# A two-block network: the wait for mixed rows taken block by block, and a next part's first row worked on at another point

## Chip, cores and metric

The kernel runs on one core of one Trainium2 chip. The metric is the device time in microseconds of one execution. Several engines work side by side on the core: TensorE (PE in the profile; its weight loads are PEld) multiplies, VectorE (DVE), ScalarE (ACT) and GpSimd (POOL) do elementwise work, SyncE (SP) issues most transfers. Each runs its own list of instructions in order, and they wait for one another through semaphores.

## What is computed

The program is two blocks one behind the other over 512 tokens of width 1024: a gated linear-attention and retention block, then a two-layer block (convolution, windowed attention). Each of those two layers ends in the part that the change touches, a gated feed-forward with 2816 hidden channels:

```python
def swiglu_ffn(x, w_up, w_down):
    gate, up = jnp.split(x @ w_up, 2, axis=-1)
    return (jax.nn.silu(gate) * up) @ w_down
...
        h = h + swiglu_ffn(rmsnorm(h, norm_ffn[l]), ffn_w_up[l], ffn_w_down[l])
    return rmsnorm(h, norm_final)
```

## The kernel before

**Products by seven instead of eight.** A float32 product is made of three passes: each operand is split into a high part (a cast) and a low part (the value less its high part), and high by high, high by low and low by high are added up. In the feed-forward the work is further cut by a Strassen-like scheme. A *pair* is a 2 by 2 block of output (two output chunks of 128 channels, two token halves of 256). `seven_products` (L2568) computes it with seven products, named `w11`, `diff`, `sum2`, `w12`, `sum1`, `w22` and `sum4`, instead of eight. Each product is 4 blocks (`HALF`) of 3 matmuls of 128x256, so 12 matmuls, and a pair is 84. Some products need sums or differences of weight blocks (made by VectorE and GpSimd), and sums or differences of input blocks, which are called *mixes*.

**Order of the pairs.** `ff_order` (L48) gives 30 pairs per layer. The 22 hidden chunks come in three parts of 8, 8 and 6. For part 0: up pairs for its chunks 0 to 7 (pairs 0 to 7), then the first up pair of the next part (pair 8), then four down pairs (9 to 12), which multiply the part's eight finished hidden chunks by the down weights. Then up pairs 13 to 19, first up pair of part 2 (pair 20), down pairs 21 to 24, up pairs 25 to 29. Part 2 goes through ordinary dense products at the end. Pairs of even number use the PSUM tensor `aps`, those of odd number `gps`.

**What a pair needs from the other engines.** ScalarE walks the same pairs (L1252 on). For pair n it casts the weights of pair n+1 (L1094, L1106, L1100, L1117, L1111), and copies four partial results of pair n out of PSUM (`copied`, L1121, steps 1 to 4). TensorE signals `product_done` for each step and waits for the copies through `partial_copied`: step 1 before `sum2`, step 3 before `sum1`, step 4 before `sum4`. Between the copies ScalarE does the silu of pair n-1 (L1214) and the high part of its hidden row (L1221, L1231 or L1235). VectorE's turn for pair n-1 is `gate_and_up` (L1975 to L1980) or `down_added` (L1986 to L1993); then it makes the low weight sums (L1845, L1850, L1855) and the next weight sums (L1838, L1840). GpSimd makes the low weights (L740, L743, L744, L746, L748).

**Hidden mixes.** After an odd hidden chunk, ScalarE casts the mixes of the two chunks (`hidden_mix_high`, L1246) and GpSimd subtracts for the low part (`hidden_mix_low`, L761, semaphore `hid_mix_low`). A part has four such mix blocks, m = 0 to 3; block 3 comes from chunks 6 and 7, that is behind pair 7. GpSimd does it behind its weights for pair 9. The products `diff` and `sum2`, `sum1` and `w22` of a down pair read them. Before pair 9 (and 21) TensorE waits for all four:

```python
if n == lead_down:
    pe.wait_ge(hid_low, mixed_at(layer_n, part + 1, 0))
    pe.wait_ge(hid_mix_low, mixes_before(layer_n, part + 1))
```

**The next part's first row.** The hidden row of pair 8 (or 20) belongs to the next part, whose first place in memory is still read by the down pairs. So it is only copied aside (`row_copy`, L1221), and worked on once the four down pairs are through: `early_high` (L1237; L1239 128x256 at the end of part 0, L1241 128x512 at the end of part 1) on ScalarE, `early_low` (L2030; L2037 and L2039, or L2034) on VectorE. Both stand at the end of the turn of pair 13 (or 25).

With two layers of two such changes of part there are four places of the first kind (pairs 9 and 21) and four of the second (pairs 13 and 25), each twice.

## Time and profile before

| | us |
|---|---|
| median of 3 runs | 1593.33 |
| lowest and highest | 1592.66, 1594.79 |
| the profiled execution, as timed | 1594.84 |
| its span in the trace | 1593.1 |
| TensorE busy | 1548.4 (97%) |
| VectorE busy | 1138.3 (71%) |
| GpSimd busy | 883.4 (55%) |
| ScalarE busy | 881.9 (55%) |

The span is 1.74 us shorter than the profiled execution's own time. The feed-forward stages lie at about 730 to 1045 us and 1235 to 1555 us of the trace. A matmul's shown length (0.28 us) is a modelled end of a pipelined instruction; the pace is read from the distance of the starts. The idle time in brackets runs from the modelled end of the matmul before. The granted clock is given as a share of 2.4 GHz.

### The profile page before, as it was taken

The page shows a single profiled execution, that of the slowest core. Times are in us where ns is not written, and L with a number is a line of the kernel's source. Part 1 is how long each engine was busy: PE and PEld are TensorE (multiplying, and loading weights), DVE is VectorE, ACT ScalarE, POOL GpSimd, SP SyncE. Part 2 cuts the span into 40 slices and gives each one's busy share as a digit, 9 for nine tenths or more (in the row PEclk, how much of TensorE's full clock was granted, in tenths as well). Part 3 has the DMA queues.
Part 4 walks back from the last instruction along what each step waited for, and adds up shares of the span by engine and source line. Part 5 has one row for each costly group of instructions (what it writes and reads, how often), then busy time and mean ns, then how long its engine had stood idle before and what let it go on. Part 6 is the DMA issues. An engine that isn't in the chain of part 4 may idle for free.

```text
span 1593.1 us, 28481 instructions
## 1 busy us (share of the span) xinstructions
PE 1548.4 (97%) x10803; PEld 1376.7 (86%) x10803; DVE 1138.3 (71%) x1782; ACT 881.9 (55%) x1480; POOL 883.4 (55%) x523
## 2 busy tenths in 40 slices
PE   6999999999999999999999999999999999999997
PEld 4888888888887878478999999988788899999996
DVE  7887687697697869877666766664666766766655
ACT  4555445455456544476664664554776665565553
POOL 1444444444445439736766776654116677677653
PEclk9999999999999999999999999999999999999999
DMA  9423322322323365612333333353112233332332
GB/s 375 139 93 88 111 93 79 118 92 81 117 92 114 114 129 148 180 53 81 106 93 106 93 106 107 105 173 103 44 41 82 92 106 107 94 105 93 106 118 69
DMA packets 53659, 173.12 MB, mean 109 GB/s; under 512 B 5403, under 2 KB 11580, under 8 KB 53052
## 3 DMA queue, kind: packets, MB, share of 16 engines
q1 hardware_dynamic: 47296, 159.90, 31.6%
q10 hardware_dynamic: 6268, 11.95, 3.3%
q8 instruction: 59, 0.97, 0.3%
q14 instruction: 36, 0.29, 0.1%
HBM read 165.48 MB, written 6.36 MB: 108 GB/s over the span
## 4 chain that ended last, share of the span: by engine, by line
PE 74%; DVE 6%; issue 4%; ACT 2%; POOL 2%; DVEq 0%; ACTq 0%; POOLq 0%
PE gps L2151 8%; PE gps L2153 8%; PE gps L2152 8%; PE gps L2586 8%; PE gps L2588 8%; PE gps L2587 8%; PE aps L2586 4%; PE aps L2587 4%; PE aps L2588 4%; PE gps L2511 2%; PE gps L2209 1%; PE gps L2210 1%; PE gps L2211 1%; POOL w_lo L665 1%; PE aps L2675 1%
## 5 line engine op out<-in xcount | busy, mean ns | idle before, releaser
L665 POOL TENSOR_TENSOR w_lo<-w_raw,w_hi 128x1024 fp32r<-128x1024 f32 x140 | 360.7, 2580 | 472.5 <-ACT w_hi L791 472.4
L2151 PE MATMUL gps<-xa_hi,w_hi 128*128 128x512 f32 x639 | 256.5, 401 | 3.9 <-DVE xa_lo L1453 3.9
L2153 PE MATMUL gps<-xa_hi,w_lo 128*128 128x512 f32 x639 | 249.8, 391 | 0.0
L2152 PE MATMUL gps<-xa_lo,w_hi 128*128 128x512 f32 x639 | 249.8, 391 | 0.0
L791 ACT CAST w_hi<-w_raw 128x1024 fp32r<-128x1024 f32 x140 | 146.3, 1045 | 98.5 <-DMA w_raw<-weights_dram 41.8
L2151 PEld LDWEIGHTS gps<-xa_hi,w_hi 128*128 128x128 f32 x639 | 120.4, 188 | 31.4 <-DVE xa_lo L1453 5.2
L746 POOL TENSOR_TENSOR w_lo<-diff,w_hi 128x512 fp32r<-128x512 f32 x60 | 77.7, 1295 | 124.0 <-ACT w_hi L1117 124.0
L2153 PEld LDWEIGHTS gps<-xa_hi,w_lo 128*128 128x128 f32 x639 | 120.3, 188 | 26.2
L1855 DVE TENSOR_TENSOR sums<-aps,sums 128x512 fp32r<-128x512 f32 x58 | 40.1, 692 | 142.1 <-ACT sums L1111 142.1
L2152 PEld LDWEIGHTS gps<-xa_lo,w_hi 128*128 128x128 f32 x639 | 120.6, 189 | 22.8
L740 POOL TENSOR_TENSOR w_lo<-w_raw,w_hi 128x512 fp32r<-128x512 f32 x60 | 91.0, 1517 | 44.8 <-ACT w_hi L1094 44.8
L2151 PE MATMUL gps<-xb_hi,w_hi 128*128 128x512 f32 x250 | 98.4, 394 | 0.0
L2153 PE MATMUL gps<-xb_hi,w_lo 128*128 128x512 f32 x250 | 97.4, 389 | 0.0
L2152 PE MATMUL gps<-xb_lo,w_hi 128*128 128x512 f32 x250 | 97.3, 389 | 0.0
L1845 DVE TENSOR_TENSOR sums<-aps,sums 128x1024 fp32r<-128x1024 f32 x58 | 70.7, 1219 | 26.5 <-ACT sums L1106 26.2
L743 POOL TENSOR_TENSOR diff<-w_raw 128x512 f32<-128x512 f32 x60 | 79.6, 1327 | 0.0
L744 POOL TENSOR_TENSOR w_lo<-w_raw,w_hi 128x512 fp32r<-128x512 f32 x60 | 78.7, 1311 | 0.0
L748 POOL TENSOR_TENSOR w_lo<-w_raw,w_hi 128x512 fp32r<-128x512 f32 x60 | 78.0, 1300 | 0.0
L2586 PE MATMUL gps<-x_blocks,w_hi 128*128 128x256 f32 x264 | 75.5, 286 | 0.0
L2588 PE MATMUL gps<-x_blocks,w_lo 128*128 128x256 f32 x264 | 74.7, 283 | 0.0
L2587 PE MATMUL gps<-x_blocks,w_hi 128*128 128x256 f32 x264 | 74.7, 283 | 0.0
L2209 PE MATMUL gps<-w_hi,xa_hi 128*128 128x256 f32 x256 | 72.8, 284 | 1.8 <-POOL w_lo L665 1.7
(495 smaller groups left out, 5135.4 us busy)
## 6 DMA issues: line engine op xcount, KB each, us to landing
w_raw<-weights_dram SPq DMA_DIRECT2D x268, 512.0 KB, 3.6
ada_w<-ada_in_dram SPq DMA_DIRECT2D x8, 1024.0 KB, 18.5
gates<-ret_tab_dram ACTq DMA_DIRECT2D x4, 1024.0 KB, 6.8
spread<-glu_scratch_dram SPq DMA_DIRECT2D x12, 270.0 KB, 5.1
rel_scratch_dram<-rel_rows ACTq DMA_DIRECT2D x1, 3072.0 KB, 34.6
x<-x_turned_dram SPq DMA_DIRECT2D x2, 1024.0 KB, 7.4
res<-xT_dram ACTq DMA_DIRECT2D x1, 2048.0 KB, 10.6
bias<-rel_scratch_dram ACTq DMA_DIRECT2D x1, 2048.0 KB, 9.5
```

The lines of the kernel that those rows point to most:

```text
L665: TT(w_lo[:, j, :], w_raw[:, j, :], w_hi[:, j, :].bitcast(F32), ALU.subtract).then_inc(lo_ready[j], 1)
L740: TT(lo["w11"], raw["w11"], hi["w11"].bitcast(F32), ALU.subtract).then_inc(first_low, 1)
L743: TT(diff[:], raw["w11"], raw["diff"], ALU.subtract).then_inc(diff_made, 1)
L744: TT(lo["w12"], raw["w12"], hi["w12"].bitcast(F32), ALU.subtract).then_inc(lo_ready[2 * s], 1)
L791: nc.scalar.copy(w_hi[:, j, :], w_raw[:, j, :]).then_inc(hi_ready[j], 1)
L2151: mm(gps[:, j, :], w_hi[:, j, w], x[0][:, k, :], start=k == 0, stop=False)
L2152: mm(gps[:, j, :], w_hi[:, j, w], x[1][:, k, :], start=False, stop=False)
L2153: last = mm(gps[:, j, :], w_lo[:, j, w], x[0][:, k, :], start=False, stop=k == blocks - 1)
L2209: mm(out, x[0][:, k, tok], wh, start=k == 0, stop=False)
L2586: mm(out, highs[s][name][:, w], x[name](k, 0), start=start and k == 0, stop=not start, **more)
L2587: mm(out, highs[s][name][:, w], x[name](k, 1), start=False, stop=not start, **more)
L2588: last = mm(out, lows[s][name][:, w], x[name](k, 0), start=False, stop=not start or k == HALF - 1, **more)
```

## The change

It has two parts.

First, `seven_products` gets an argument `mixes`. For the first down pair of a part (9 and 21) it holds how many mixes were there before the part, and each block k of `diff` waits for mix k alone. The wait for all mixes ahead of the pair goes. And, as was so already for the very first pair of a layer (`lead`), `diff` and `sum2` are cut behind their third block: three blocks of `diff`, three of `sum2`, then the last of `diff`, then the last of `sum2`. `product_done` for step 2 is now signalled behind the last block of `diff`, so 33 matmuls into the pair instead of 24; that for step 3 stays at 36.

Second, `early_high` moves from the end of ScalarE's turn for pair 13 (25) to between its copies 2 and 3, and `early_low` from the end of VectorE's turn, behind the weight sums for the pair after next, to ahead of `last_sum_low`.

```diff
--- before.py
+++ after.py
@@ -1267,6 +1267,9 @@
                     copied(f, 2, hbuf[:, 2 * s + 1, TH:], UP_SUM[s])
                     if kind == "up":
                         hidden_high(1 - s, part, k)
+                    if kind == "down" and k == KC // 2 - 1:
+                        act.wait_ge(tile_done[2 * (1 - s) + 1], up + (n - 1) // 2 + 2)
+                        early_high(part + 1)
                     copied(f, 3, hbuf[:, 2 * s + 1, 0:TH], UP_ROW[s])
                     if n == 0:
                         act.wait_ge(sq_used, USED[norm] + 4)
@@ -1282,9 +1285,6 @@
                     if n == 0:
                         rms_finish(norm, bank=NORM_BANK)
                         first_copy(f + 1, I1, s1)
-                    if kind == "down" and k == KC // 2 - 1:
-                        act.wait_ge(tile_done[2 * (1 - s) + 1], up + (n - 1) // 2 + 2)
-                        early_high(part + 1)
                     if kind == "up" and part < MIXED_PARTS and k % 2 == 1:
                         hidden_mix_high(f - 1, part, k // 2)
                 kind, part, k = FF_ORDER[-1]
@@ -2052,12 +2052,12 @@
                         last_sum(f + 1, 1 - s)
                     if kind == "up":
                         hidden_low(1 - s, part, k)
+                    if kind == "down" and k == KC // 2 - 1:
+                        early_low(part + 1)
                     if n + 1 < FF_PAIRS:
                         last_sum_low(f + 1, 1 - s)
                     if n + 2 < FF_PAIRS:
                         two_sums(up + (n + 2) // 2, f + 2, s)
-                    if kind == "down" and k == KC // 2 - 1:
-                        early_low(part + 1)
                 kind, part, k = FF_ORDER[-1]
                 gate_and_up(FF_PAIRS - 1, part, k)
                 hidden_low((FF_PAIRS - 1) % 2, part, k)
@@ -2565,7 +2565,7 @@
                         "diff": lambda k, h: mix[:, 1, k, h, :], "w22": lambda k, h: mix[:, 2, k, h, :],
                         "sum2": lambda k, h: mix[:, 3, k, h, :]}
 
-            def seven_products(f, I, s, x, lead=None):
+            def seven_products(f, I, s, x, lead=None, mixes=None):
 
                 def input_made(name, k):
 
@@ -2582,6 +2582,8 @@
                     for k in range(k0, k1):
                         if lead is not None:
                             input_made(name, k)
+                        if mixes is not None and name == "diff":
+                            pe.wait_ge(hid_mix_low, mixes + k + 1)
                         w = slice(k * P, (k + 1) * P)
                         mm(out, highs[s][name][:, w], x[name](k, 0), start=start and k == 0, stop=not start, **more)
                         mm(out, highs[s][name][:, w], x[name](k, 1), start=False, stop=not start, **more)
@@ -2597,14 +2599,15 @@
                     pe.wait_ge(block_ready, KC * lead + KC - 2)
                 product("w11", UP_ROW[s], start=True).then_inc(product_done, 1)
                 pe.wait_ge(diff_low, f + 2)
-                split = HALF - 1 if lead is not None else HALF
+                in_turn = lead is not None or mixes is not None
+                split = HALF - 1 if in_turn else HALF
                 last = product("diff", UP_SUM[s], start=True, k1=split)
-                if lead is None:
+                if not in_turn:
                     last.then_inc(product_done, 1)
                 pe.wait_ge(partial_copied, 4 * f + 1)
                 pe.wait_ge(sum_low, 2 * f + 1)
                 last = product("sum2", UP_ROW[s], k1=split)
-                if lead is not None:
+                if in_turn:
                     product("diff", UP_SUM[s], start=True, k0=split).then_inc(product_done, 1)
                     last = product("sum2", UP_ROW[s], k0=split)
                 last.then_inc(product_done, 1)
@@ -2639,9 +2642,9 @@
                     for n in range(lead_down // 2 * 2, last_down // 2 * 2 + 2):
                         if n == lead_down:
                             pe.wait_ge(hid_low, mixed_at(layer_n, part + 1, 0))
-                            pe.wait_ge(hid_mix_low, mixes_before(layer_n, part + 1))
                         kind, _, _ = FF_ORDER[n]
-                        seven_products(f0 + n, up + n // 2, n % 2, own_x if kind == "down" else x)
+                        seven_products(f0 + n, up + n // 2, n % 2, own_x if kind == "down" else x,
+                                       mixes=mixes_before(layer_n, part) if n == lead_down else None)
                     at = last_down // 2 + 1
                 quads(at, FF_PAIRS // 2)
                 n = FF_PARTS[-1]
```

No instruction is added or removed but waits. Line numbers behind L1269 shift by 3 at most (L2586 to L2588 become L2588 to L2590). These are rows of the order in which the instructions stand on an engine.

TensorE at the start of pair 9 of the first layer, before (two rows of pair 8 first, `hid_bottom` and `hid_top` are the hidden rows, `xa_mix` the mixes):

```order
L2587 MATMUL gps<-x_blocks,sums 128x256
L2588 MATMUL gps<-x_blocks,sums 128x256
L2586 MATMUL gps<-hid_bottom,w_hi 128x256 [waits evicted2,evicted3,rows_free,first_low,hid_mix_low,hid_low]
L2587 MATMUL gps<-hid_bottom,w_hi 128x256
L2588 MATMUL gps<-hid_bottom,w_lo 128x256
L2586 MATMUL gps<-hid_top,w_hi 128x256
```

After, from the end of `w11` into `diff`:

```order
L2589 MATMUL gps<-hid_top,w_hi 128x256
L2590 MATMUL gps<-hid_top,w_lo 128x256
L2588 MATMUL gps<-xa_mix,w_hi 128x256 [waits hid_mix_low,diff_low]
L2589 MATMUL gps<-xa_mix,w_hi 128x256
L2590 MATMUL gps<-xa_mix,w_lo 128x256
L2588 MATMUL gps<-xa_mix,w_hi 128x256 [waits hid_mix_low]
L2589 MATMUL gps<-xa_mix,w_hi 128x256
```

The wait `hid_mix_low` stands no longer at the first matmul of `w11` but at each block of `diff`.

TensorE in the same pair, where `diff` (`w_hi`, `w_lo`) ends and `sum2` (`sums`) begins, before:

```order
L2588 MATMUL gps<-xa_mix,w_lo 128x256
L2586 MATMUL gps<-xa_mix,w_hi 128x256
L2587 MATMUL gps<-xa_mix,w_hi 128x256
L2588 MATMUL gps<-xa_mix,w_lo 128x256
L2586 MATMUL gps<-xa_mix,sums 128x256 [waits sum_low,partial_copied]
L2587 MATMUL gps<-xa_mix,sums 128x256
```

After, from the end of `sum2`'s third block through the two last blocks to `w12`:

```order
L2589 MATMUL gps<-xa_mix,sums 128x256
L2590 MATMUL gps<-xa_mix,sums 128x256
L2588 MATMUL gps<-xa_mix,w_hi 128x256 [waits hid_mix_low]
L2589 MATMUL gps<-xa_mix,w_hi 128x256
L2590 MATMUL gps<-xa_mix,w_lo 128x256
L2588 MATMUL gps<-xa_mix,sums 128x256
L2589 MATMUL gps<-xa_mix,sums 128x256
L2590 MATMUL gps<-xa_mix,sums 128x256
L2588 MATMUL gps<-hid_bottom,w_hi 128x256 [waits lo_ready2]
```

The fourth block of `diff`, with its wait, stands behind three blocks of `sum2`.

ScalarE in the turn of pair 13 (first layer), from its first copy to the weights for pair 15, before:

```order
L1121 COPY gps<-gps 128x256 [waits product_done,evicted1]
L1106 CAST sums<-aps 128x1024 [waits sum_made,tile_done1]
L1121 COPY hbuf<-gps 128x256 [waits product_done] x2
L1100 CAST w_hi<-w_raw 128x512 [waits tile_done1,raw_in1]
L1117 CAST w_hi<-diff 128x512 [waits tile_done1,diff_made]
L1121 COPY gps<-gps 128x256 [waits product_done]
L1111 CAST sums<-aps 128x512 [waits sum_made]
L1239 CAST hid_bottom<-hbuf 128x256 [waits tile_done1]
L1094 CAST w_hi<-w_raw 128x1024 [waits tile_done2,raw_in2]
```

After:

```order
L1121 COPY gps<-gps 128x256 [waits product_done,evicted1]
L1106 CAST sums<-aps 128x1024 [waits sum_made,tile_done1]
L1121 COPY hbuf<-gps 128x256 [waits product_done]
L1239 CAST hid_bottom<-hbuf 128x256 [waits tile_done1]
L1121 COPY hbuf<-gps 128x256 [waits product_done]
L1100 CAST w_hi<-w_raw 128x512 [waits tile_done1,raw_in1]
L1117 CAST w_hi<-diff 128x512 [waits tile_done1,diff_made]
L1121 COPY gps<-gps 128x256 [waits product_done]
L1111 CAST sums<-aps 128x512 [waits sum_made]
```

The cast L1239 moved ahead of the third copy (the second `hbuf<-gps` copy).

VectorE in the same turn, with the rows taken away and put in:

```order
 L1845 TENSOR_TENSOR sums<-aps,sums 128x1024 [waits sum_high]
 L1850 TENSOR_TENSOR aps<-w_raw,aps 128x512 [waits sum_low]
-L1855 TENSOR_TENSOR sums<-aps,sums 128x512 [waits sum_high]
-L1838 TENSOR_TENSOR aps<-w_raw 128x512 [waits sum_low,raw_in2,raw_in3]
-L1840 TENSOR_TENSOR aps<-aps,w_raw 128x512 [waits sum_made]
 L2037 TENSOR_TENSOR hid_bottom<-hbuf,hid_bottom 128x256 [waits hid_high]
 L2039 TENSOR_TENSOR hbuf<-hbuf 128x256 [waits hid_low]
+L1855 TENSOR_TENSOR sums<-aps,sums 128x512 [waits sum_high]
+L1838 TENSOR_TENSOR aps<-w_raw 128x512 [waits sum_low,raw_in2,raw_in3]
+L1840 TENSOR_TENSOR aps<-aps,w_raw 128x512 [waits sum_made]
 L1975 TENSOR_TENSOR sq<-gps,rstd 128x512 [waits tile_done3]
```

The two instructions of `early_low` stand now ahead of the low part of the last weight sum (L1855) and of the sums for pair 15 (L1838, L1840), and `gate_and_up` of pair 13 (L1975) follows these sums directly.

## Rows read from the trace of the kernel before

**Rows 1.** page, section 1: busy us, share of the span, instructions

```profile
PE 1548.4 (97%) x10803; PEld 1376.7 (86%) x10803; DVE 1138.3 (71%) x1782; ACT 881.9 (55%) x1480; POOL 883.4 (55%) x523
```

**Rows 2.** waits of TensorE: total us, times, longest us

```profile
PE gps L2586 <- issue: 7.6, 4, 1.9
...
PE aps L2586 <- ACT gps L1121: 3.8, 5, 1.2
```

**Rows 3.** TensorE's timeline, first place: start, length, instruction, [idle before, its releaser]

```profile
823.63 0.28 PE L2588 MATMUL gps<-x_blocks,sums 128*128 128x256 f32 x1
825.81 0.36 PE L2586 MATMUL gps<-hid_bottom,w_hi 128*128 128x256 f32 x1 [1.90 <-issue]
...
826.60 0.38 PE L2586 MATMUL gps<-hid_top,w_hi 128*128 128x256 f32 x1
...
830.14 0.28 PE L2588 MATMUL gps<-xa_mix,w_lo 128*128 128x256 f32 x1
...
837.45 0.28 PE L2586 MATMUL aps<-hid_bottom,w_hi 128*128 128x256 f32 x1
```

**Rows 4.** timeline of GpSimd and ScalarE at the first place

```profile
822.96 2.75 POOL L761 TENSOR_TENSOR xa_mix<-hbuf,xa_mix 128x1024 fp32r<-128x1024 f32 x1 [0.73 <-ACT xa_mix L1246]
...
824.86 0.63 ACT L1214 ACTIVATE sq<-sq 128x512 f32<-128x512 f32 x1 [1.03 <-DVE sq L1975]
```

**Rows 5.** stretches of 15 us: length, TensorE busy (matmuls), clock, DMA share, GB/s

```profile
900.00:915.00 15.00, 15.00 (x127) 1.00 0.28 89
823.00:838.00 15.00, 13.10 (x97) 0.89 0.30 85
949.00:964.00 15.00, 13.10 (x98) 0.89 0.31 87
1329.00:1344.00 15.00, 13.10 (x109) 1.00 0.35 107
...
880.00:895.00 15.00, 13.77 (x115) 1.00 0.24 71
```

**Rows 6.** timeline of ScalarE in the pair before the first place

```profile
815.37 0.36 ACT L1121 COPY gps<-aps 128x256 f32<-128x256 f32 x1
...
818.20 0.37 ACT L1121 COPY hbuf<-aps 128x256 f32<-128x256 f32 x1 [0.58 <-PE aps L2588]
```

**Rows 7.** timeline of VectorE at the second place

```profile
872.32 0.69 DVE L1850 TENSOR_TENSOR aps<-w_raw,aps 128x512 f32<-128x512 f32 x1
875.99 0.69 DVE L1855 TENSOR_TENSOR sums<-aps,sums 128x512 fp32r<-128x512 f32 x1 [2.98 <-ACT sums L1111]
...
877.55 0.70 DVE L1840 TENSOR_TENSOR aps<-aps,w_raw 128x512 f32<-128x512 f32 x1
878.16 0.78 DVE L2037 TENSOR_TENSOR hid_bottom<-hbuf,hid_bottom 128x256 fp32r<-128x256 f32 x1
878.97 1.40 DVE L2039 TENSOR_TENSOR hbuf<-hbuf 128x256 f32<-128x256 f32 x1
880.30 0.68 DVE L1975 TENSOR_TENSOR sq<-gps,rstd 128x512 f32<-128x512 f32 x1
```

**Rows 8.** timeline of ScalarE at the second place

```profile
870.77 0.37 ACT L1121 COPY hbuf<-gps 128x256 f32<-128x256 f32 x1
872.22 0.37 ACT L1121 COPY hbuf<-gps 128x256 f32<-128x256 f32 x1 [1.07 <-PE gps L2588]
...
881.54 0.36 ACT L1121 COPY gps<-aps 128x256 f32<-128x256 f32 x1
```

**Rows 9.** timeline of GpSimd at the second place

```profile
873.70 1.29 POOL L746 TENSOR_TENSOR w_lo<-diff,w_hi 128x512 fp32r<-128x512 f32 x1 [2.60 <-ACT w_hi L1117]
```

**Rows 10.** instructions of one line: min/median/max ns; and one undisturbed subtraction

```profile
L1239 ACT CAST hid_bottom<-hbuf x2: 418/418/418, 875.8 to 1380.8; 128x256 fp32r<-128x256 f32 x2
...
L1241 ACT CAST xa_hi<-hbuf x1: 634/634/634, 1001.9 to 1001.9; 128x512 fp32r<-128x512 f32 x1
...
808.81 0.41 DVE L2025 TENSOR_TENSOR hbuf<-aps,hbuf 128x256 f32<-128x256 f32 x1
```

## The prediction

> **What bounds the kernel now.** I read the busy shares first. TensorE is busy 97% of the span, VectorE 71%, the others 55% [rows 1]. So in the feed-forward nothing is gained but where TensorE stands still or runs slow. Next I read TensorE's waits. Two groups in the feed-forward's line stand out: four waits of 1.9 us each, 7.6 us, put down to "issue", and five for ScalarE's copy L1121, 3.8 us, the longest 1.2 us [rows 2].
>
> The timeline shows what the first group is. Pair 8 ends with a matmul that starts at 823.63; the first of pair 9 starts at 825.81 [rows 3]. GpSimd's last mix (L761) runs from 822.96 to 825.71 [rows 4], so the wait ends 0.10 us behind it. It is the wait for the mixes, whatever the profile calls it. The undisturbed pace is 127 matmuls in 15 us, 0.12 us from start to start [rows 5], so the next matmul was due at 823.75 and came 2.06 us late.
>
> The stall is not the whole loss. From 826.60 to 830.14 there are 17 matmuls, 0.21 us apart [rows 3], and the granted clock of that stretch of 15 us is 0.89 on the mean [rows 5]: for some 3.5 us TensorE ran at the lower of its two levels, 1.2 GHz in place of 2.4. It had stood idle 1.9 us just before. A pair of 84 matmuls should take 84 x 0.12 = 10.08 us; pair 9 took from 823.75 to 837.45, 13.70 us [rows 3], so 3.6 us too long.
>
> The same in counts: the stretch at the first place holds 97 matmuls where 127 fit, 30 x 0.12 = 3.60 us lost. The second place lost 29 x 0.12 = 3.48 us. The third, whose clock stayed at 1.00, lost 18 x 0.12 = 2.16 us [rows 5]. The fourth (1454 to 1469 us) has the count and the clock of the second, 3.48 us. Together **12.7 us**, of which about 4.2 us is the slow clock.
>
> **First part: the wait by blocks.** Removed: the wait ahead of `w11`. With it gone pair 9 can start at 823.75. The rows of `w11`, 12 matmuls, last until 825.19, and three blocks of `diff` until 823.75 + 21 x 0.12 = 826.27. Mixes 0 to 2 were made two or more pairs ago. Three blocks of `sum2` last until 827.35, and only there is mix 3 needed. It is ready at 825.71 [rows 4]: GpSimd's L761 hangs on ScalarE's cast of the mixes and on pair 9's weights, neither of which waits for this stall. 1.6 us to spare, so the price of the new waits is nothing. Were the cover gone, each microsecond of a later mix beyond these 1.6 would come back.
>
> What is late next? Three things, in the order in which TensorE meets them.
> - The first copy, due at 826.27 instead of 826.63, because `sum2` now comes three matmuls earlier. ScalarE's silu of pair 8 starts at 824.86 and takes 0.63 [rows 4]. In pair 8, which started 10.08 us before, at 813.67, the copy started at 815.37, 1.70 us in, and took 0.36 [rows 6]. The same in pair 9 gives 825.45 to 825.81. Spare: 0.46 us.
> - The third copy. Step 2 is signalled 33 matmuls into the pair, at 827.71, instead of 24; step 3 at 36 as before. In pair 8 the third copy started 0.21 us behind its signal (813.67 + 4.32 = 817.99; 818.20 [rows 6]). With the same lag copy 2 starts at 827.92, takes 0.37, then comes the row copy of 128x512, for which I take the cast of that size, 0.63 [rows 10], then copy 3, 0.37: ready at 829.29. `sum1` is due at 823.75 + 48 x 0.12 = 829.51. Spare: 0.22 us, the tightest. I take 0 and keep 0 to 0.3 us a place, 1.2 us in all, as the upper end.
> - The weights of pair 10, due at 833.83 and behind. GpSimd starts them at 825.7 as it does now, since it did not wait for TensorE there. The low part of `diff` needs ScalarE's casts behind copy 3, so 829.3 + 1.25 (two casts of 0.63), then 1.3 on GpSimd [rows 9]: 831.9, needed at 835.27. No price.
>
> No DMA is issued at another point; the queue's share is 0.30 in these stretches against 0.28 in an undisturbed one [rows 5], so a pair that comes 3.6 us sooner is no load.
>
> With the idle time gone the slow clock should go: in these rows it follows the 1.9 us of idling at three of four places. So I take the whole 12.7 us. The bounds: 12.7 - 4.2 = 8.5 if the low clock stayed, and 13.2 above, since a count is good to one matmul, 0.12 us at each of four places.
>
> **Second part: the first row moved.** In pair 14 (start 837.45 + 4 x 10.08 = 877.77) `sum2` is due at 880.65. The first copy ran from 881.54 to 881.90 [rows 8]. ScalarE did it behind the silu, and that hangs on VectorE's L1975, which started only at 880.30, behind L2037 and L2039 [rows 7]. These took 0.78 and 1.40 us beside busy GpSimd, where a subtraction of the same size takes 0.41 [rows 10]. Cost: the stretch from 880 holds 115 matmuls of 127, 12 x 0.12 = 1.44 us [rows 5], and the second layer has the same count (1385 to 1400 us): 2.88 us.
>
> Moved ahead, the two instructions fall into VectorE's hole from 873.01 (end of L1850) to 875.99, 2.98 us [rows 7]. Their input is ready: ScalarE's cast, 0.42 (0.63 in the larger form) [rows 10], comes behind copy 2, whose end is 871.14, and copy 3 did not start before 872.22 [rows 8], so it fits in ScalarE's own hole of 1.07 and is done by 871.8 at the latest. The two instructions last between 2 x 0.41 = 0.82 and 2.14 (878.16 to 880.30, the old place). GpSimd starts L746 at 873.70 [rows 9], after the first of them; I take about 1.2, and both ends fit. Then L1855, L1838 and L1840 keep their times, L1975 starts at 878.16 in place of 880.30, and the copy ends at 881.90 - 2.14 = 879.76, 0.89 us before it is due. The wait goes whole.
>
> A page says more on that neighbourhood. The Trainium skill, SBUF — State Buffer, Who interferes with whom, has a VectorE instruction with two SBUF inputs and a GpSimd instruction that reads SBUF exclude each other for a whole instruction. The trace agrees in kind (0.78 and 1.40 against 0.41). By the rule both could wait for a GpSimd instruction of 1.3 us each, 3.4 us in all, 0.4 beyond the hole; that is inside the 0.89 us to spare, so the sum stays, and only the margin shrinks.
>
> The two places at the end of part 1 lose little: 3.8 us less 2 x 1.2 leaves 1.4 us for three waits [rows 2], not all of them there. I take 0.1 each, 0.2; the bounds are 0 and 1.4.
>
> **Sum.** 12.7 + 2.9 + 0.2 = 15.8 us. The profiled execution took 1594.84 us, so 1579.0. It is 1.5 us above the median of the runs shown (1593.33), and I give the forecast against the median: **1577.5 us**, 0.990 of before. As 0.2% (3.2 us) is about what a measurement can tell, this is well outside.
>
> **The rivals.**
> 1. *The low clock stays.* The drop is not tied to this idle time but comes again within the stage, near each change of part. For: it came at only three of four equal stalls, so something beside the stall decides. Against: outside these stalls the stretches show 1.00, also where TensorE waited 1.2 us (880 to 895) [rows 5]. Price: the first place lost 12 matmuls' time more than the third, 1.44 us; three of them 4.3 us: 1581.8 us.
> 2. *ScalarE's chain in pair 9 is late.* 0.22 us to spare before `sum1`, 0.46 before `sum2`. If a signal or a copy takes 0.5 us more than I think, TensorE stops 0.3 us at each place; and if the row copy waits for VectorE, more. Price 1 to 3 us: 1579.5 us.
> 3. *The change does not do what it says.* The 1.9 us end with something else that comes at the same time as mix 3, so pair 9 still stands. Against: the end 0.10 us behind L761. The second part alone leaves 1593.3 - 3.1 = 1590.2 us.
> 4. *Slower.* The pauses are what lets the clock stay high: a TensorE that works without a pause gets the lower level from time to time in the 60 pairs. Each such episode costs 1.44 us, so it decides from 11 more than now (15.8 / 1.44). One in every third pair is 20 x 1.44 = 28.8 us: 1606.3 us. Against: 15 us with all 127 matmuls at 1.00 [rows 5], and the drops stand behind idling, not behind work. The Trainium skill, TensorE: Matmul & The Clock Gate, Part 1, says that activity releases the throttle and that its peak-current limit does not trip with one or two busy cores; here one core is busy and the rows agree, which is why I give this little.
>
> **How the numbers follow.** The forecast, all stalls and drops gone: 0.76. Rival 1: 0.09. Rival 2: 0.08. Rival 3: 0.03. Rival 4: 0.04. The forecast's own spread is the runs' (the three shown span 2.1 us) and the ends of the terms (upper end 1.2 us for the chain, 1.2 us of gain for the later second places). The range reaches from 1575.0 over rivals 1 and 2 to 1583.0 us and leaves out rivals 3 and 4 and a little of the rest. Faster by over 0.2%: 0.76 + 0.09 + 0.08 = 0.93. Within 0.2%: rival 3, 0.03. Slower: rival 4, 0.04.
>
> **What would show it right or wrong.** In the trace of the changed kernel the four waits of 1.9 us before a down pair are gone, and any matmul of pair 9 that waits names a block of `diff` or the copies. Stretches around these places hold about 127 matmuls in 15 us at a clock of 1.00. VectorE's L2037 and L2039 stand in front of L1855, last 0.8 to 2.1 us, and L1855 has less idle time in front; L1975 follows L1840 with no gap, and pair 14 has no wait before `sum2`. TensorE's busy time falls by about the slow clock's 4 us, and the rest of the gain is idle time. The prediction is wrong if the fourth block of `diff` waits for L761, if copy 3 of pair 9 starts later than about 5.3 us into the pair, or if low-clock stretches show up between pairs with no stall before them.

## The result

| | median us | lowest to highest | runs |
|---|---|---|---|
| before | 1592.99 | 1592.02 to 1594.79 | 4 |
| changed | 1578.05 | 1576.66 to 1578.58 | 4 |

The ratio is 0.9904, with a 95% interval from 0.9886 to 0.9921: faster by 14.9 us. A second comparison gave 0.991 [0.9893, 0.9926]. The forecast was 1577.5 us, in a range from 1575.0 to 1583.0.

The profiled execution of the changed kernel took 1578.51 us, its span is 1576.7 us, 16.4 us shorter than before. The page's first section (busy us, share, instructions) answers [rows 1]:

```profile
PE 1544.0 (98%) x10803; PEld 1372.8 (87%) x10803; DVE 1134.5 (72%) x1782; ACT 881.7 (56%) x1480; POOL 884.3 (56%) x523
```

TensorE is busy for 4.4 us less, for the same number of instructions. That this equals what the slow clock cost is chance. Within the two feed-forward stages the busy time fell by 6.4 us, from 616.1 to 609.7. Of that 4.4 us are the slow clock, and 2.0 us are modelled ends of matmuls and slow first steps at the waits that went. The stages ahead of the first feed-forward were 1.9 us busier. The idle time within the two stages fell by 10.4 us, from 14.9 to 4.5. So the two stages are 16.8 us shorter, and the others 0.4 us longer. TensorE's waits (total, times, longest), beside [rows 2]:

```profile
PE gps L2588 <- ACT hbuf L1121: 2.9, 2, 1.5
...
PE aps L2588 <- ACT gps L1121: 1.0, 1, 1.0
```

The four waits of 7.6 us put down to "issue" are gone from the list, and of the five for the copy into `gps` one is left, at the start of a layer, with which the change has nothing to do. The first row, a wait of 1.46 us in pair 1 of each layer, was there before too.

The stretches of 15 us around the four places of the first kind and, last, one of the second kind (length, TensorE busy, matmuls, granted clock, DMA share, GB/s), beside [rows 5]:

```profile
820.00:835.00 15.00, 15.00 (x127) 1.00 0.39 117
945.00:960.00 15.00, 15.00 (x128) 1.00 0.28 100
1325.00:1340.00 15.00, 15.00 (x128) 1.00 0.34 105
1450.00:1465.00 15.00, 15.00 (x127) 1.00 0.42 132
874.00:889.00 15.00, 15.00 (x127) 1.00 0.33 106
```

Each holds the 127 or 128 matmuls that an undisturbed stretch held, where before there were 97, 98, 109 and 98, and 115 in the stretches that the prediction counted. The clock is 1.00.

**Inside pair 9.** GpSimd's last mix and TensorE's starts of `w11`, `diff` and the fourth block of `diff`:

```profile
823.35 2.82 POOL L761 TENSOR_TENSOR xa_mix<-hbuf,xa_mix 128x1024 fp32r<-128x1024 f32 x1 [0.72 <-ACT xa_mix L1246]
```

```profile
824.14 0.28 PE L2588 MATMUL gps<-hid_bottom,w_hi 128*128 128x256 f32 x1
...
825.58 0.28 PE L2588 MATMUL gps<-xa_mix,w_hi 128*128 128x256 f32 x1
...
827.74 0.28 PE L2588 MATMUL gps<-xa_mix,w_hi 128*128 128x256 f32 x1
```

The pair begins 0.12 us behind pair 8's last start, the mix is ready at 826.17 and first needed at 827.74: 1.57 us to spare, the prediction had 1.64. ScalarE's copies 1, 2, the row copy and copy 3 of that pair:

```profile
825.84 0.36 ACT L1121 COPY gps<-gps 128x256 f32<-128x256 f32 x1
...
828.30 0.37 ACT L1121 COPY hbuf<-gps 128x256 f32<-128x256 f32 x1 [1.18 <-PE gps L2590]
828.57 0.59 ACT L1221 COPY hbuf<-aps 128x512 f32<-128x512 f32 x1
829.05 0.39 ACT L1121 COPY hbuf<-gps 128x256 f32<-128x256 f32 x1
```

Copy 3 is through at 829.44. `sum1` was due 48 matmuls in, at 824.14 + 5.76 = 829.90. So 0.46 us were to spare, where the prediction had 0.22 (copy 1, through at 826.20 and needed at 826.66, had the 0.46 foretold): the row copy takes 0.59 instead of 0.63, and the next copy starts before the one in front is through.

**Inside pairs 13 and 14.** VectorE, beside [rows 7], ScalarE, beside [rows 8], and GpSimd, beside [rows 9]:

```profile
869.69 0.42 DVE L2037 TENSOR_TENSOR hid_bottom<-hbuf,hid_bottom 128x256 fp32r<-128x256 f32 x1
870.14 0.42 DVE L2039 TENSOR_TENSOR hbuf<-hbuf 128x256 f32<-128x256 f32 x1
872.76 0.69 DVE L1855 TENSOR_TENSOR sums<-aps,sums 128x512 fp32r<-128x512 f32 x1 [2.19 <-ACT sums L1111]
873.59 0.70 DVE L1838 TENSOR_TENSOR aps<-w_raw 128x512 f32<-128x512 f32 x1
874.32 0.70 DVE L1840 TENSOR_TENSOR aps<-aps,w_raw 128x512 f32<-128x512 f32 x1
874.93 0.68 DVE L1975 TENSOR_TENSOR sq<-gps,rstd 128x512 f32<-128x512 f32 x1
```

```profile
867.81 0.41 ACT L1239 CAST hid_bottom<-hbuf 128x256 fp32r<-128x256 f32 x1
...
876.24 0.36 ACT L1121 COPY gps<-aps 128x256 f32<-128x256 f32 x1
```

```profile
870.47 1.29 POOL L746 TENSOR_TENSOR w_lo<-diff,w_hi 128x512 fp32r<-128x512 f32 x1 [2.60 <-ACT w_hi L1117]
```

L2037 and L2039 take 0.42 each instead of 0.78 and 1.40, in a hole in which GpSimd is idle but for the last 0.1 us. L1855 has 2.19 us of idling left in front. L1975 stands right behind L1840. The first copy of pair 14 ends at 876.60, 0.82 us before `sum2` is due (pair 14 starts at 824.14 + 5 x 10.08 = 874.54; + 2.88 = 877.42).

### The profile page after: what moved, and what is told of

Read it like the earlier page. It is cut to its first block, busy times and chain, and to the rows that moved or that the text cites. A ratio compares the mean times of both kernels' runs of the same rounds, so it can differ in the third digit from the quotient of the medians.

```text
span 1576.7 us, 28481 instructions
## 1 busy us (share of the span) xinstructions
PE 1544.0 (98%) x10803; PEld 1372.8 (87%) x10803; DVE 1134.5 (72%) x1782; ACT 881.7 (56%) x1480; POOL 884.3 (56%) x523
## 4 chain that ended last, share of the span: by engine, by line
PE 79%; DVE 3%; issue 2%; ACT 2%; POOL 2%; DVEq 0%; ACTq 0%; POOLq 0%
PE gps L2151 9%; PE gps L2153 9%; PE gps L2152 9%; PE gps L2588 8%; PE gps L2590 8%; PE gps L2589 8%; PE aps L2588 4%; PE aps L2589 4%; PE aps L2590 4%; PE gps L2511 2%; PE gps L2209 2%; PE gps L2210 1%; PE gps L2211 1%; POOL w_lo L665 1%; PE aps L2678 1%
## 5 line engine op out<-in xcount | busy, mean ns | idle before, releaser
L665 POOL TENSOR_TENSOR w_lo<-w_raw,w_hi 128x1024 fp32r<-128x1024 f32 x140 | 361.1, 2584 | 472.5 <-ACT w_hi L791 472.4
L1855 DVE TENSOR_TENSOR sums<-aps,sums 128x512 fp32r<-128x512 f32 x58 | 40.1, 692 | 138.4 <-ACT sums L1111 138.4
L740 POOL TENSOR_TENSOR w_lo<-w_raw,w_hi 128x512 fp32r<-128x512 f32 x60 | 92.7, 1545 | 41.6 <-ACT w_hi L1094 41.5
L1845 DVE TENSOR_TENSOR sums<-aps,sums 128x1024 fp32r<-128x1024 f32 x58 | 70.8, 1221 | 17.1 <-ACT sums L1106 16.8
L743 POOL TENSOR_TENSOR diff<-w_raw 128x512 f32<-128x512 f32 x60 | 78.5, 1308 | 0.0
L748 POOL TENSOR_TENSOR w_lo<-w_raw,w_hi 128x512 fp32r<-128x512 f32 x60 | 78.1, 1301 | 0.0
L2588 PE MATMUL gps<-x_blocks,w_hi 128*128 128x256 f32 x264 | 75.5, 286 | 0.0
L2590 PE MATMUL gps<-x_blocks,w_lo 128*128 128x256 f32 x264 | 74.7, 283 | 0.0
```

Of the source, the lines that this page charges most:

```text
L665: TT(w_lo[:, j, :], w_raw[:, j, :], w_hi[:, j, :].bitcast(F32), ALU.subtract).then_inc(lo_ready[j], 1)
L740: TT(lo["w11"], raw["w11"], hi["w11"].bitcast(F32), ALU.subtract).then_inc(first_low, 1)
L743: TT(diff[:], raw["w11"], raw["diff"], ALU.subtract).then_inc(diff_made, 1)
L2588: mm(out, highs[s][name][:, w], x[name](k, 0), start=start and k == 0, stop=not start, **more)
L2590: last = mm(out, lows[s][name][:, w], x[name](k, 0), start=False, stop=not start or k == HALF - 1, **more)
```

## Experiments

Every kernel was timed beside the kernel before on the same chip, and ratios are to that. Times of different calls differ by a microsecond or two beyond the medians, since the stages ahead of the feed-forward vary: the first matmul of the first feed-forward's pair 0 starts between 727.3 and 733.0 us in the traces. So what the traces show between two matmuls is the finer measure. "Lost" below is the time that a pair took, from the last start of the pair ahead to its own last start, over 84 x 0.12 us. It holds the wait and the slower first steps behind it: a wait that the prediction counts as 2.06 us between two starts is 2.13 us lost.

### The two parts by themselves

The first kernel has the first part alone: `early_high` and `early_low` stand where they were before.

```diff
@@ ScalarE's and VectorE's turns, against the changed kernel
-if kind == "down" and k == KC // 2 - 1:
-    act.wait_ge(tile_done[2 * (1 - s) + 1], up + (n - 1) // 2 + 2)
-    early_high(part + 1)
 copied(f, 3, hbuf[:, 2 * s + 1, 0:TH], UP_ROW[s])
...
+if kind == "down" and k == KC // 2 - 1:
+    act.wait_ge(tile_done[2 * (1 - s) + 1], up + (n - 1) // 2 + 2)
+    early_high(part + 1)
...
-if kind == "down" and k == KC // 2 - 1:
-    early_low(part + 1)
 if n + 1 < FF_PAIRS:
     last_sum_low(f + 1, 1 - s)
 if n + 2 < FF_PAIRS:
     two_sums(up + (n + 2) // 2, f + 2, s)
+if kind == "down" and k == KC // 2 - 1:
+    early_low(part + 1)
```

> The first part of the change alone: the mixes waited for block by block with the two last blocks at the end; the next part's first row is worked on in its old place. Theory (the two parts remove different waits and their gains add): the wait before the down pair and its slow clock are gone, 12.9 us, and pair 14's wait of 1.2 us stays in each layer, 3.0 us with its pace. Time 1578.05 + 3.1 = 1581.1 us, two waits of about 1.2 us for ScalarE's copy before sum2 in pair 14, none before pair 9, granted clock 1.00 around pair 9. Rival (a pair that starts 3.6 us sooner runs into the same late row, so the parts don't add and the old wait grows): over 1583 us, the waits before sum2 longer than 1.5 us.

Measured: 1583.86 us (1582.16 to 1584.61), ratio 0.9928 [0.9909, 0.9947]. TensorE's waits for the copy:

```profile
PE aps L2588 <- ACT gps L1121: 3.8, 5, 1.2
```

The same as [rows 2] to the digit: five, the longest 1.2 us. Lost in pair 14: 1.48 us in each layer, as before; in pair 26: 0.44 us, as before; none ahead of pairs 9 and 21. The wait did not grow, and the trace bears out the theory of two independent waits. The median by itself lies in the rival's range, but the kernel before took 1595.29 us beside it, and 0.9928 of 1592.99 is 1581.5 us, the theory's figure.

The second kernel has the second part alone: the wait for all four mixes stands ahead of `w11` again.

```diff
 pe.wait_ge(hid_low, mixed_at(layer_n, part + 1, 0))
+pe.wait_ge(hid_mix_low, mixes_before(layer_n, part + 1))
...
-               mixes=mixes_before(layer_n, part) if n == lead_down else None)
+               mixes=None)
```

> The second part of the change alone: the next part's first row is worked on in the new place, all four mixes are waited for before the down pair as before. Theory: 1592.99 - 3.1 = 1589.9 us; four waits of 1.9 us stay, the waits of 1.2 us in pair 14 are gone, the slow clock still comes behind most of the four waits. Rival (the gain of this part is taken back since the long wait before had given the other engines time): no difference from before, 1592 to 1593.5 us.

Measured: 1589.97 us (1586.67 to 1593.55), ratio 0.9964 [0.9948, 0.998]. The ratio makes this 5.7 us, and the theory's 3.1 us (0.998) lies at the edge of the interval. Its stretches around the four places of the first kind and one of the second:

```profile
820.00:835.00 15.00, 13.10 (x110) 1.00 0.30 92
945.00:960.00 15.00, 13.11 (x110) 1.00 0.31 102
1325.00:1340.00 15.00, 13.10 (x110) 1.00 0.29 90
1450.00:1465.00 15.00, 13.11 (x110) 1.00 0.29 105
874.00:889.00 15.00, 15.00 (x128) 1.00 0.44 129
```

The waits in pair 14 are gone (128 matmuls from 874). The four waits of 1.9 us are there, 2.1 us lost at each. But 110 matmuls, not 97, and the clock is 1.00 at all four: in this execution it did not fall at any of them. So the stall does not bring the low clock each time, and the question was open how much of the 12.7 us of the first part is the chip's chance. Its span, 1586.6 us, is 6.5 us under that of before: 3.9 us for the second part's places and 4.4 us of low clock, less 1.9 us by which its first feed-forward began later.

### Is the cut of diff needed?

```diff
@@
-    in_turn = lead is not None or mixes is not None
+    in_turn = lead is not None
```

> The changed kernel without the cut: each block of diff waits for its own mix, but diff is done whole, four blocks, and then sum2, as in every other down pair. Theory (the wait ahead of w11 was the whole matter, and w11 with three blocks of diff is cover enough): mix 3 is ready at 826.17 in the trace after, the fourth block of diff would be due at 824.14 + 21 x 0.12 = 826.66, so nothing waits: 1578 us, within 0.2% of the changed kernel, no wait in pair 9. Rival (the cut is needed): a wait for GpSimd's mix of up to 0.5 us in each of four pairs, 1580 us, and more where the clock falls behind it.

Measured: 1578.56 us (1576.87 to 1579.3), ratio 0.989 [0.987, 0.9909], the same as the change. GpSimd's last mix, and TensorE at the start of `diff`'s fourth block:

```profile
824.19 2.80 POOL L761 TENSOR_TENSOR xa_mix<-hbuf,xa_mix 128x1024 fp32r<-128x1024 f32 x1 [0.72 <-ACT xa_mix L1246]
```

```profile
827.50 0.28 PE L2588 MATMUL gps<-xa_mix,w_hi 128*128 128x256 f32 x1
```

Ready at 826.99, needed at 827.50: 0.51 us to spare, and nothing waits. The two last blocks at the end add cover that the wait by blocks does not need. The cut's gain is nothing, and it costs nothing either. The two places where the prediction saw little to spare, the first and the third copy, are places that the cut itself moves closer: in this trace they end 0.82 and 0.87 us before they are needed, with the cut 0.46 and 0.46.

### How late must the wait stand?

```diff
@@
-                pe.wait_ge(hid_mix_low, mixes + k + 1)
+                pe.wait_ge(hid_mix_low, mixes + HALF)
@@
-    in_turn = lead is not None or mixes is not None
+    in_turn = lead is not None
```

> As the one without the cut, but the first block of diff waits for all four mixes. So TensorE waits 12 matmuls later than in the kernel before. Theory: diff is due at 824.14 + 1.44 = 825.58, mix 3 is there at 826.17 + 0.10: a wait of 0.7 us at each of four places, 2.8 us, 1580.9 us, and if the low clock follows only idling as long as 1.9 us, the clock stays at 1.00. Rival (any idling at this place brings the low clock, as at three of four places before): 1.4 us more at three or four places, 1585 to 1586.5 us.

Measured: 1585.25 us (1581.33 to 1586.38), ratio 0.9929 [0.9908, 0.9951]. The median lies at the rival's figure, the ratio (0.9929 of 1592.99 is 1581.7 us) and the trace at the theory's. The last matmul of `w11` and the first of `diff`:

```profile
829.19 0.28 PE L2590 MATMUL gps<-hid_top,w_lo 128*128 128x256 f32 x1
830.02 0.36 PE L2588 MATMUL gps<-xa_mix,w_hi 128*128 128x256 f32 x1 [0.54 <-POOL xa_mix L761]
```

0.76 to 0.78 us lost at each of the four places, 3.1 us, no low clock in any. In this trace the first feed-forward began 3.7 us later than in the changed kernel's, and that and the 3.1 us make up the whole difference of the two spans, 6.8 us. Most of the 3.7 us is one wait ahead of the feed-forward, for GpSimd's `w_lo` (L665): 5.0 us in all in this trace, 1.7 in the changed kernel's. The edit does not touch that stage; why it differs stays open. So moving the wait behind 12 matmuls alone takes out 1.4 of the 2.1 us, and waiting by blocks takes out the rest.

### Which half of the second part?

ScalarE's cast in the new place, VectorE's two subtractions in the old one:

```diff
-if kind == "down" and k == KC // 2 - 1:
-    early_low(part + 1)
 if n + 1 < FF_PAIRS:
     last_sum_low(f + 1, 1 - s)
 if n + 2 < FF_PAIRS:
     two_sums(up + (n + 2) // 2, f + 2, s)
+if kind == "down" and k == KC // 2 - 1:
+    early_low(part + 1)
```

> The changed kernel with VectorE's half of the second part put back: ScalarE's cast (L1239, L1241) in the new place, VectorE's subtractions (L2037, L2039, L2034) in the old one. Theory (the wait in pair 14 comes from VectorE's two subtractions that stand ahead of the next gate): they still run beside busy GpSimd, about 2.1 us, and the two waits of 1.2 us are back: 1578.05 + 3.0 = 1581.1 us. Rival (ScalarE's cast at the end of its turn was what made the copy late): no wait in pair 14, 1578 us.

Measured: 1581.13 us (1580.03 to 1582.11), ratio 0.9923 [0.9906, 0.9939]. Both waits in pair 14 are back, 1.49 us lost in each layer. VectorE and GpSimd:

```profile
872.97 0.79 DVE L2037 TENSOR_TENSOR hid_bottom<-hbuf,hid_bottom 128x256 fp32r<-128x256 f32 x1
873.79 1.40 DVE L2039 TENSOR_TENSOR hbuf<-hbuf 128x256 f32<-128x256 f32 x1
```

```profile
871.78 1.69 POOL L740 TENSOR_TENSOR w_lo<-w_raw,w_hi 128x512 fp32r<-128x512 f32 x1 [0.72 <-ACT w_hi L1094]
873.43 1.48 POOL L743 TENSOR_TENSOR diff<-w_raw 128x512 f32<-128x512 f32 x1
```

0.79 and 1.40 us again. Each of the two starts while a GpSimd instruction runs and ends 0.3 us behind it: L2037 behind L740, which ends at 873.47, and L2039 behind L743, which ends at 874.91. Moving ScalarE's cast alone brings nothing in pair 14, and 0.1 us in pair 26 (0.32 us lost instead of 0.45).

VectorE's subtractions in the new place, ScalarE's cast in the old one:

```diff
-if kind == "down" and k == KC // 2 - 1:
-    act.wait_ge(tile_done[2 * (1 - s) + 1], up + (n - 1) // 2 + 2)
-    early_high(part + 1)
 copied(f, 3, hbuf[:, 2 * s + 1, 0:TH], UP_ROW[s])
...
+if kind == "down" and k == KC // 2 - 1:
+    act.wait_ge(tile_done[2 * (1 - s) + 1], up + (n - 1) // 2 + 2)
+    early_high(part + 1)
```

> The other half put back: ScalarE's cast in the old place at the end of its turn, VectorE's subtractions in the new one, where they now wait for that cast. Theory (what stands behind a waiting instruction on VectorE is the late sums and the next gate): the cast is done at 873.0 in the frame of the trace after, so L2037 starts 3.4 us later than 869.69, L1855 and all behind it 1.2 to 2 us later, and the first copy of pair 14 is 0.5 to 1.3 us late for sum2; the same at the end of part 1: 2 to 5 us in all, 1580 to 1583 us. Rival (the 2.19 us that VectorE idles before L1855 cover it): 1578 us.

Measured: 1582.8 us (1582.67 to 1584.65), ratio 0.9935 [0.9919, 0.9952]. VectorE and GpSimd:

```profile
873.04 0.43 DVE L2037 TENSOR_TENSOR hid_bottom<-hbuf,hid_bottom 128x256 fp32r<-128x256 f32 x1 [3.28 <-ACT hid_bottom L1239]
...
874.67 1.22 DVE L1838 TENSOR_TENSOR aps<-w_raw 128x512 f32<-128x512 f32 x1
...
876.53 0.68 DVE L1975 TENSOR_TENSOR sq<-gps,rstd 128x512 f32<-128x512 f32 x1
```

```profile
874.04 1.29 POOL L740 TENSOR_TENSOR w_lo<-w_raw,w_hi 128x512 fp32r<-128x512 f32 x1 [1.04 <-ACT w_hi L1094]
```

VectorE waits 3.28 us for the cast (the hole and 0.3 us more), the two subtractions are as short as in the changed kernel, but everything behind is late: L1975 starts 1.6 us later than in the changed kernel. And L1838, whose inputs both lie in SBUF, now takes 1.22 instead of 0.70 us: it starts within GpSimd's L740 and ends 0.56 us behind it. TensorE loses 0.97 us in pair 14 and 1.17 us in pair 26, 4.3 us in all, where before the pairs 26 lost 0.45 each. So the two halves need each other: the cast has to move so that VectorE's hole can be used.

### The low clock

Before all this the low clock had come at three of four waits. A longer wait, in the changed kernel, ahead of the same pairs:

```diff
@@
+                pe.wait_ge(first_low, f0 + n + 2)
```

> The changed kernel with one more wait ahead of pairs 9 and 21: for GpSimd's first low weights of the next pair (L740 behind L761), so that TensorE stands about 3.3 us instead of the 1.9 us of before, and everything else is as changed. 3.3 x 4 = 13.2 us of idling. Theory (how long TensorE idles decides how often the clock falls; 1.9 us did it at three of four places in one trace and at none in another): now at all four places, 1.4 us or more each: 1578.05 + 13.2 + 5.8 = 1597 us. Rival (the low clock is a matter of the single execution and not of this stall): at none to two places, 1591 to 1594 us.

Measured: 1596.02 us (1593.16 to 1598.13), ratio 1.0012 [1.0002, 1.0021]. The four stretches:

```profile
820.00:835.00 15.00, 11.89 (x88) 0.89 0.21 71
945.00:960.00 15.00, 11.88 (x87) 0.89 0.22 70
1325.00:1340.00 15.00, 11.88 (x90) 0.91 0.22 72
1450.00:1465.00 15.00, 11.88 (x99) 1.00 0.24 72
```

3.34 us lost at the fourth place by standing, and the clock fell at three of four (0.89, 0.89, 0.91), for 1.4 to 1.5 us more each (4.74, 4.84 and 4.82 us lost). The price was about right, "at all four places" was not.

Then the kernel before, unchanged, twice more.

> The kernel before, unchanged, for a second trace. The first trace had the low clock behind three of its four waits of 1.9 us, the trace of the second part alone behind none of the same four, that with 3.3 us behind three. Theory (whether the clock falls behind such a wait is a matter of the single execution): again four waits of 1.9 us and 2.06 us lost at each, and another number of low stretches than three, or the three at other places. Rival (it is fixed by the kernel's own timing, and the second part of the change took it away): low stretches behind the first, second and fourth wait again.

Measured: 1592.61 us.

```profile
820.00:835.00 15.00, 13.10 (x109) 1.00 0.34 106
945.00:960.00 15.00, 13.11 (x98) 0.89 0.33 105
1325.00:1340.00 15.00, 13.10 (x110) 1.00 0.34 107
1450.00:1465.00 15.00, 13.11 (x110) 1.00 0.36 107
```

> The kernel before, unchanged, for a third trace. Expected as for the second; the spans of the three should differ by about 1.5 us for each low stretch more or less.

Measured: 1595.23 us.

```profile
945.00:960.00 15.00, 13.10 (x97) 0.89 0.33 99
...
1450.00:1465.00 15.00, 13.10 (x97) 0.89 0.30 101
```

(The first and the third place of that trace have 109 and 110 matmuls at 1.00.) One fall in the first of the two, at the second place; two in the other, at the second and fourth. The half of the rival that has fixed places is out. A fall in the traces of before cost 1.5 us (3.59 to 3.62 us lost against 2.12 to 2.13). The spans were 1593.1 (three falls), 1590.8 (one) and 1593.5 us (two). So the span does not follow the falls alone: of the 2.7 us between the last two one fall is 1.5, and 1.1 us is a later begin of the feed-forward.

All traces together:

| waits ahead of pairs 9 and 21 | places | falls of the clock |
|---|---|---|
| none (changed, changed again, first part alone, no cut, each half of part two, copies first) | 28 | 0 |
| 0.8 us lost (wait at diff) | 4 | 0 |
| 2.1 us lost, before three times | 12 | 6 |
| 2.1 us lost, second part alone | 4 | 0 |
| 3.3 us lost (long wait) | 4 | 3 |

Elsewhere in the feed-forward no trace shows a fall. That takes in 24 waits in pair 1 (all kernels but copies first, 1.7 us with the slow step behind) and ten in pair 14 (before three times, first part alone, ScalarE's half; 1.5 us lost).

The timed runs say how often the clock fell too, since the mean granted clock of each is on record. One fall, some 3.5 us at half the clock, takes 0.0011 off the mean of a run (3.5 x 0.5 / 1593). The kernel before has 0.9930 (35 runs in three comparisons), the kernels without a wait ahead of pairs 9 and 21 have 0.9957 (28 runs), the wait at `diff` 0.9958 (4), the second part alone 0.9944 (8) and the long wait 0.9926 (10). Against the 0.9957 that makes, as estimates, about 2.4 falls in an execution of the kernel before, 1.2 with the second part alone and 2.8 with the long wait. (The start and the end of the program run at the low clock as well, for a time that varies from run to run, so a single run tells little.)

So the other half of that rival, that the second part of the change took the falls away, is not out: with the second part alone the clock fell about half as often behind waits of the same length, 0.9944 against 0.9930 in the same comparison (single runs 0.993 to 0.995 against 0.992 to 0.994). By these estimates that is about 1.2 falls of 1.5 us, and with the 3.9 us of the second part's own places it gives the 5.7 us measured for that kernel. Why it fell less often there, no run shows.

The changed kernel once more, for the first row of that table:

> The changed kernel again, beside the kernel before on the same chip. Theory: no wait in the feed-forward beyond those at its start, and no low clock there: a ratio of 0.990. If the low clock were free to come without a wait, some stretch of the feed-forward would show under 1.00 here or in one of the other traces without these waits.

Measured: 1578.4 us (1576.73 to 1579.9), ratio 0.991 [0.9893, 0.9926].

```profile
945.00:960.00 15.00, 15.00 (x128) 1.00 0.29 102
...
1450.00:1465.00 15.00, 15.00 (x127) 1.00 0.40 131
```

### A step further

In the changed kernel two waits of 1.46 us are left in pair 1.

```diff
@@
+        if n == 1:
+            copied(f, 2, hbuf[:, 2 * s + 1, TH:], UP_SUM[s])
+            copied(f, 3, hbuf[:, 2 * s + 1, 0:TH], UP_ROW[s])
@@
-        copied(f, 2, hbuf[:, 2 * s + 1, TH:], UP_SUM[s])
+        if n != 1:
+            copied(f, 2, hbuf[:, 2 * s + 1, TH:], UP_SUM[s])
@@
-        copied(f, 3, hbuf[:, 2 * s + 1, 0:TH], UP_ROW[s])
+        if n != 1:
+            copied(f, 3, hbuf[:, 2 * s + 1, 0:TH], UP_ROW[s])
```

> The changed kernel with one more edit: in ScalarE's turn for pair 1 of each layer the copies 2 and 3 stand ahead of the cast of the next weight sums (L1106) and of the hidden row (L1221, L1235), which are late there since the silu before them has to load its table (1.28 us). In the trace after TensorE waits 1.46 us for copy 3 before sum1 of pair 1, and loses 1.6 us with its pace, in each layer. Theory (the order on ScalarE is the cause): copy 3 ends about 747.4 instead of 749.12, TensorE was due at 747.54: the wait goes, 1578.05 - 3.3 = 1574.8 us. Rival (the sums and the row, 0.64 us later now, are late for pair 2 and the wait comes there): 1576 to 1578 us, with a new wait in pair 2.

Measured: 1576.02 us (1575.16 to 1579.41), ratio 0.9893 [0.9876, 0.9909]. Of the 1.7 us lost at that wait in pair 1 of each layer 1.6 us are gone. But the rival is right: pair 2 now loses 0.92 us before its `sum2`, at a place that was free before. TensorE there and VectorE ahead of it (line numbers are 5 higher in this kernel: L1843 is the L1838 of the changed one, L1980 its L1975):

```profile
755.14 0.38 PE L2593 MATMUL aps<-xb_mix,sums 128*128 128x256 f32 x1 [0.67 <-ACT gps L1121]
```

```profile
751.22 1.52 DVE L1843 TENSOR_TENSOR aps<-w_raw 128x512 f32<-128x512 f32 x1
...
753.39 0.68 DVE L1980 TENSOR_TENSOR sq<-gps,rstd 128x512 f32<-128x512 f32 x1
```

VectorE's sum of weights L1843, both inputs in SBUF, takes 1.52 us with GpSimd's L748 running when it begins, and the gate behind it comes late. The gain by the traces is 1.57 - 0.92 = 0.65 us a layer, 1.3 us; against the changed kernel the intervals overlap, so by the times it is not told from it.

## Why the prediction was right

**What bounds the kernel.** Right: TensorE's time fell by what its waits and its slow matmuls held. No other engine was given less to do.

**First part, the wait.** 2.06 us at each of four places and 0.07 for the slow first step behind it, 8.5 us: right, shown by the stretches and by the second part alone, in which they stay. That the "issue" in the profile is the wait for mix 3 is shown by moving it: with the wait at `diff` it is called by its name, 0.5 to 0.6 us for `xa_mix` and `xb_mix` L761.

**First part, the low clock.** The mechanism was right: without the wait no fall is seen. The price was taken from one trace, 4.2 us for its three falls. The three traces of before have 3, 1 and 2, and the mean clocks of 35 runs give about 2.4 falls (an estimate), 2.4 x 1.48 = 3.6 us. So the term was 0.6 us too large, and that it was so near owes something to which trace was taken: one with a single fall would have given 1.5 us. Its bounds were too narrow as well. Four falls are 5.9 us and make the part 14.4 us, where the prediction had 13.2 as its upper end.

**Second part.** 1.44 us a place by counts, 1.48 by starts: right. That VectorE and not ScalarE was late is shown by the two halves. The subtractions were taken as 1.2 us together; they measured 0.84, since both began while GpSimd was idle. The copy was foretold 0.89 us before it was due and came 0.82 us before.

**Places at the end of part 1.** Mis-sized, inside the stated bounds. The prediction took 0.1 us each; pair 26 lost 0.45 us in each layer in all three traces of before, and nothing in the changed one. The wait itself is 0.20 us in the profile, but between the two starts there are 0.48 us instead of 0.12, and the first steps behind are slow:

```profile
1006.56 0.28 PE L2588 MATMUL aps<-xb_mix,w_lo 128*128 128x256 f32 x1
1007.04 0.38 PE L2586 MATMUL aps<-xb_mix,sums 128*128 128x256 f32 x1 [0.20 <-ACT gps L1121]
```

So this term is 0.9 us, not 0.2.

**The sum.** By the trace of before: 8.5 + 4.4 (its three falls) + 3.0 + 0.9 = 16.8 us in the feed-forward stages, and the spans differ by 16.4, since the other stages took 0.4 us longer in the changed kernel's trace. With the estimated mean of the falls it is 8.5 + 3.6 + 3.0 + 0.9 = 16.0 us. The forecast had 15.8: the clock's term was 0.6 us too large and the last term 0.7 us too small, and these two errors took each other out. The medians give 14.9 us, 14.0 in the second comparison, and 16.7 for the kernel without the cut, whose trace loses as much as the changed kernel's to 0.1 us. Of the 1 to 2 us between 16.0 and the first two, no trace shows where they lie; the stages ahead of the feed-forward vary by more than that. That the forecast came within 0.6 us is in part luck.

TensorE's busy time was foretold to fall by the slow clock's 4 us, and it fell by 4.4 us, but the account above shows that this was not the slow clock alone.

**The rivals.** Rival 1, the low clock stays though the waits go: out, none in 28 places. Rival 2, ScalarE's chain is late: not seen, 0.46 us were to spare, and 0.8 us without the cut. Rival 3, the wait is not what it seems: out. Rival 4, no pause brings the clock down: out, 28 pairs in a row (2 to 29) of each layer without loss, at 1.00, in both traces of the changed kernel; no fall came without a pause ahead of it. What decides whether a pause brings one stays open.

## What to carry to other kernels

When an engine that bounds the kernel waits for a late input ahead of a group of products, look at which product first reads it. Waiting there, and by blocks, may cover the whole wait with work that stands anyway, and the reordering that goes further may bring nothing. A term that one trace shows as a state of the chip, such as the clock behind a pause, should be priced by how often it comes, from more than one trace, before it goes into a sum whole; the mean clock of every timed run tells it too. And a short wait costs more than the idle time that the profile gives it: the distance between the starts, and the pace of the first steps behind, are the measure.

## What the runs showed of the hardware

The granted clock fell from 2.4 to 1.2 GHz in some executions behind TensorE's idling of 1.9 us and not in others of the same kernel, at the same place: 6 of 12 places in three traces of the kernel before, none of 4 with the second part alone. Behind losses of 3.3 us it fell at 3 of 4, behind 0.8 us at none of 4, behind 34 waits of 1.5 to 1.7 us in pairs 1 and 14 at none, and in 28 places without a wait at none. A fall cost 1.4 to 1.5 us.

A VectorE instruction on two SBUF inputs took 0.42 us (128x256) or 0.70 us (128x512) where it began ahead of GpSimd's next one, and up to 1.40 and 1.52 us where a GpSimd instruction was running. There it ended 0.3 us (128x256) or 0.56 us (128x512) behind the end of GpSimd's. The other way round GpSimd waits: in the changed kernel L1838 starts at 873.59 and takes 0.70 us, and GpSimd's L740, begun at 873.75, takes 1.70 instead of 1.29 us. So the one that begins first keeps its length. Where VectorE's instructions of that kind stood ahead of a gate, the delay went on to ScalarE and TensorE; moved by a few microseconds, the same instructions fell ahead of a GpSimd instruction or into it: the sum L1838 took 0.70 us in the turn of pair 13 of the changed kernel and 1.22 with only VectorE's half moved; in the turn of pair 1 it took 0.72 and, with the copies first, 1.52. The Trainium skill, SBUF — State Buffer, Who interferes with whom, says that such an instruction contends with one of GpSimd's that reads SBUF, and the traces agree.
